# Narrow FoX key tiles in pairs in one score bank, and values multiplied two units behind their scores

## The reference, cut to what matters

```
u = RMSNorm(h); [q,k,v,z]_swa, [q,k,v,z,f]_fox, gate_swa, gate_fox = u @ w_in
y_swa = attention with sinks, ALiBi and a chunked window (8 heads, 2 key heads) * silu(z_swa)
log_f = log_sigmoid(ff + b_forget);  c = cumsum(log_f)
logits[t,s] = q[t].k[s] / 8 + c[t] - c[s],  s <= t;  y_fox = softmax(logits) @ v * silu(z_fox)   (8 heads)
h + RMSNorm((sigmoid(gate_swa) * (y_swa @ w_up_swa) + sigmoid(gate_fox) * (y_fox @ w_up_fox)) @ w_out)
```

## Time and profile before

| | us |
|---|---|
| median of 3 runs | 812.93 |
| lowest, highest | 811.78, 816.03 |
| the profiled execution, its own time | 811.67 |
| its span, first to last instruction | 809.9 |
| mean granted TensorE clock | 0.999 |

### The profile page before, as it was taken

The page is one execution under the profiler, slowest core; times in us unless marked ns, Lnnn a source line. Parts: engine busy times, 40 slices in busy tenths (PEclk is TensorE's granted clock), DMA queues, the critical chain, the costliest instruction groups (busy, mean ns, idle before and its releaser), DMA issues.

```text
span 809.9 us, 11838 instructions
## 1 busy us (share of the span) xinstructions
PE 789.2 (97%) x4058; PEld 624.0 (77%) x4058; DVE 481.1 (59%) x1006; ACT 315.4 (39%) x650; POOL 340.7 (42%) x287
## 2 busy tenths in 40 slices
PE   6999999999999999999999999999998999999996
PEld 4998889888888888888888865655554788878885
DVE  6835258577787777645646366677777634441222
ACT  6534022343334333333334337666767122231111
POOL 1132300765445535444445325758766335512221
PEclk9999999999999999999999999999999999999999
DMA  9344114479955435344344598999800665352222
GB/s 279 107 142 112 51 41 132 135 188 246 215 141 152 111 91 152 99 122 117 99 129 121 140 280 217 232 230 232 192 1 14 224 179 157 104 207 79 104 78 79
DMA packets 127813, 116.02 MB, mean 143 GB/s; under 512 B 29693, under 2 KB 102221, under 8 KB 127754
## 3 DMA queue, kind: packets, MB, share of 16 engines
q1 hardware_dynamic: 126456, 111.53, 51.8%
q10 hardware_dynamic: 1298, 3.74, 1.2%
HBM read 81.99 MB, written 34.96 MB: 144 GB/s over the span
## 4 chain that ended last, share of the span: by engine, by line
PE 88%; issue 4%; POOL 3%; DVE 3%; ACT 2%; DVEq 0%; ACTq 0%; POOLq 0%
PE PS L1986 21%; PE PS L1987 21%; PE PS L1988 21%; PE PS L2270 4%; PE PS L2272 4%; PE PS L2271 4%; PE PS L2192 3%; PE PS L2131 2%; POOL acc L1307 2%; PE PS L2172 1%; PE PS L2207 1%; PE PS L2173 1%; PE PS L2223 1%; PE PS L2018 1%; ACT p_fox L1480 1%
## 5 line engine op out<-in xcount | busy, mean ns | idle before, releaser
L1234 POOL TENSOR_TENSOR ops<-s_sum,ops 128x512 fp32r<-128x512 f32 x64 | 91.3, 1436 | 96.7 <-ACT ops L1336 96.7
L1234 POOL TENSOR_TENSOR ops<-raw,ops 128x512 fp32r<-128x512 f32 x48 | 67.9, 1416 | 118.8 <-ACT ops L1336 118.4
L1986 PE MATMUL PS<-t_hi,ops 128*128 128x512 f32 x256 | 100.1, 391 | 0.0
L1988 PE MATMUL PS<-t_hi,ops 128*128 128x512 f32 x256 | 99.9, 390 | 0.0
L1987 PE MATMUL PS<-t_lo,ops 128*128 128x512 f32 x256 | 99.9, 390 | 0.0
L1307 POOL TENSOR_TENSOR acc<-acc,p_fox 128x400 f32<-128x400 f32 (+5 forms) x76 | 61.4, 830 | 6.9 <-ACT p_fox L1480 5.8
L1480 ACT ACTIVATE p_fox<-PS,neg_c_col 128x512 f32<-128x512 f32 (+5 forms) x112 | 54.3, 536 | 13.0 <-PE PS L2178 8.5
L1804 DVE TENSOR_TENSOR z_tmp<-u,PS 128x512 f32<-128x512 f32 x48 | 32.9, 686 | 42.7 <-PE PS L1988 23.5
L1336 ACT ACTIVATE ops<-s_sum 128x512 fp32r<-128x512 f32 x64 | 39.4, 623 | 47.9 <-DVE s_sum L1588 42.8
L1988 PEld LDWEIGHTS PS<-t_hi,ops 128*128 128x128 f32 x256 | 48.1, 188 | 10.3
L1457 ACT ACTIVATE stage_b<-z_tmp,half_bg 128x512 f32<-128x512 f32 x32 | 23.2, 725 | 82.9 <-DVE z_tmp L1804 82.9
(11 more groups left out here) (237 smaller groups left out, 2040.9 us busy)
## 6 DMA issues: line engine op xcount, KB each, us to landing
raw<-in_w_in_dram SPq DMA_DIRECT2D x34, 512.0 KB, 5.3
g_dram<-stage_b SPq DMA_DIRECT2D x32, 256.0 KB, 2.0
tanh_g<-g_dram SPq DMA_DIRECT2D x16, 512.0 KB, 4.0
x_all<-in_x_dram SPq DMA_DIRECT2D x8, 512.0 KB, 7.3
raw<-in_w_in_dram SPq DMA_DIRECT2D x16, 256.0 KB, 4.7
q_dram<-stage_b SPq DMA_DIRECT2D x16, 256.0 KB, 2.8
q_swa_dram<-stage_b SPq DMA_DIRECT2D x16, 256.0 KB, 2.9
z_dram<-stage_b SPq DMA_DIRECT2D x16, 256.0 KB, 2.0
```

What stands on the lines that cost most here:

```text
L1234: nc.gpsimd.tensor_tensor(ops[:, i % OPS, 1], op_source(p, name), ops[:, i % OPS, 0].bitcast(F32), ALU.subtract).then_inc(op_ready, 1)
L1986: pe.matmul(dst, hi_w, hi, start=first, stop=False)
L1988: return pe.matmul(dst, lo_w, hi, start=False, stop=last)
```

## The change

A unit may now hold two narrow tiles side by side in one score bank: 400 with 16 columns, and 272 with 144. Half 0 has three units, half 1 seven, so a pair has 10 and the stage 40. Scores, exponentials, values and adds stay one instruction (or set) for each tile; semaphores are counted by unit. The mask matmul now comes right behind its head's scores. The last tile of half 0 has 16 keys, not 128. The adds (a step of their own now, `acc`) stay one unit behind the scores; the values on PE are two units behind (LAG). Items get one unit each, from unit 2 to unit 33. The tables of turns are set for 10 units; den stays two units behind the last tile.

```diff
+LAG = 2
 PROB_RING = 3
 FIRST_SLOT = 2
-REC_UNITS = ((4, 5, 6, 7, 8), (2, 3, 4, 5, 5))
-SECOND_LOADS = ((2, "load_queries", 0), (3, "load_keys", 0), (4, "load_values", 0), (8, "load_z", 0),
-                (9, "load_keys", 1), (10, "load_queries", 1), (11, "load_values", 1), (12, "load_z", 1))
+UNITS = (((0,), (1, 4), (2, 3)), ((0,), (1,), (2,), (3,), (4,), (5, 8), (6, 7)))
+REC_UNITS = ((4, 5, 6, 7, 7), (2, 3, 3, 4, 4))
+SECOND_LOADS = ((2, "load_queries", 0), (2, "load_keys", 0), (3, "load_values", 0), (6, "load_z", 0),
+                (7, "load_keys", 1), (8, "load_queries", 1), (9, "load_values", 1), (9, "load_z", 1))
 EARLY_UPS = 2
-SPLIT_TURNS = ((1, 0, 0, 1), (2, 1, 0, 1), (3, 2, 0, 1), (4, 3, 0, 1), (6, PAIRS + 2, 0, 2), (9, 0, 1, 2), (9, 1, 1, 2),
-               (10, 2, 1, 2), (10, 3, 1, 2), (11, PAIRS, 0, 2), (12, PAIRS + 1, 0, 2))
-NEXT_LOADS = ((1, "load_queries", None), (3, "load_keys", None), (5, "load_values", None), (6, "load_z", None))
+SPLIT_TURNS = ((1, 0, 0, 1), (2, 1, 0, 1), (2, 2, 0, 1), (3, 3, 0, 1), (4, PAIRS + 2, 0, 2), (7, 0, 1, 2), (7, 1, 1, 2),
+               (8, 2, 1, 2), (8, 3, 1, 2), (9, PAIRS, 0, 2), (9, PAIRS + 1, 0, 2))
+NEXT_LOADS = ((1, "load_queries", None), (2, "load_keys", None), (3, "load_values", None), (4, "load_z", None))
+UP_TURNS = (2, 4, 6, 8)
...
-    keys = min(P, LENGTH - P * i)
+    keys = min(P, r0 + w + N_META - P * i)
...
+def unit_tiles(q, tiles):
+
+    out, at = [], 0
+    for i in tiles:
+        r0, w, keys, masked, shift = key_tile(q, i)
+        out.append((i, at, r0, w, keys, masked, shift))
+        at += w
+    assert at <= BANK
+    return out
...
-    units = [(j, q, i) for j in range(PAIRS) for q in range(2) for i in range(4 * q + 5)]
+    units = [(j, q, tiles) for j in range(PAIRS) for q in range(2) for tiles in UNITS[q]]
     per = len(units) // PAIRS
-    spread = len(units) - 8 - FIRST_SLOT
+    spread = ITEMS
...
-        if u:
-            pj, pq, pi = units[u - 1]
-            steps.append(dict(kind="values", j=pj, q=pq, i=pi, u=u - 1, first=pi == 0, last=pi == 4 * pq + 4))
+        for kind, back in (("acc", 1), ("values", LAG)):
+            if u >= back:
+                steps.append(of_unit(kind, u - back))
...
-        if split_ups and not slot and (j >= 2):
+        if j == 2 and x in UP_TURNS:
...
+    for kind, back in (("values", 2), ("acc", 1), ("values", 1)):
+        steps.append(of_unit(kind, len(units) - back))
...
+                        for k, (i, at_, r0, w, keys, masked, shift) in enumerate(st["tiles"]):
+                            c0 = r0 - BANK * q
+                            dst = acc[0:keys, f % 2, h, c0:c0 + w]
+                            tile = p_fox[0:keys, n % PT_RING, at_:at_ + w]
+                            if q == 0 and i == 0:
+                                nc.gpsimd.tensor_copy(dst, tile).then_inc(acc_done["pool"], 1)
+                                continue
+                            other = p_fox[:, (n - 2) % PT_RING, :] if (q, i) == (1, 1) else dst
+                            if (n, k) in acc_before:
+                                pool.wait_ge(*acc_before[n, k])
+                            nc.gpsimd.tensor_tensor(dst, other, tile, ALU.add).then_inc(acc_done["pool"], 1)
...
-                        nc.scalar.activation(p_fox[0:keys, n % PT_RING, 0:w],
-                                             PS[0:keys, S_BANKS[n % S_RING], 0:w], ACT.Exp,
-                                             bias=neg_c_col[0:keys, i, 2 * j + h:2 * j + h + 1],
-                                             scale=1.0).then_inc(fox_exp, 1)
+                        for i, at_, r0, w, keys, masked, shift in st["tiles"]:
+                            ins = nc.scalar.activation(p_fox[0:keys, n % PT_RING, at_:at_ + w],
+                                                       PS[0:keys, S_BANKS[n % S_RING], at_:at_ + w], ACT.Exp,
+                                                       bias=neg_c_col[0:keys, i, 2 * j + h:2 * j + h + 1], scale=1.0)
+                        ins.then_inc(fox_exp, 1)
...
-                        pe.matmul(dst, KA[n][:, h, kk], QA[n][:, h, tok], start=True, stop=False)
-                        ins = pe.matmul(dst, KB[n][:, h, kk], QB[n][:, h, tok], start=False, stop=not masked)
-                        if not masked:
-                            ins.then_inc(tile_done, 1)
-                    if masked:
-                        for h in range(2):
-                            pe.matmul(PS[0:keys, S_BANKS[(2 * u + h) % S_RING], 0:masked], causal[:, 0:keys],
-                                      ident_b[:, shift:shift + masked], start=False, stop=True).then_inc(tile_done, 1)
+                        for i, at_, r0, w, keys, masked, shift in st["tiles"]:
+                            tok, kk = slice(r0, r0 + w), slice(P * i, P * i + keys)
+                            bank = PS[0:keys, S_BANKS[x % S_RING], :]
+                            dst = bank[:, at_:at_ + w]
+                            pe.matmul(dst, KA[n][:, h, kk], QA[n][:, h, tok], start=True, stop=False)
+                            ins = pe.matmul(dst, KB[n][:, h, kk], QB[n][:, h, tok], start=False, stop=not masked)
+                            if masked:
+                                ins = pe.matmul(bank[:, at_:at_ + masked], causal[:, 0:keys],
+                                                ident_b[:, shift:shift + masked], start=False, stop=True)
+                        ins.then_inc(tile_done, 1)
...
-                        ins = pe.matmul(PS[h * HEAD:(h + 1) * HEAD, Y_BANKS[f % 2], c0:c0 + w],
-                                        VF[j % 2][0:keys, i, h * HEAD:(h + 1) * HEAD],
-                                        p_fox[0:keys, x % PT_RING, 0:w], start=st["first"], stop=st["last"])
+                    for k, (i, at_, r0, w, keys, masked, shift) in enumerate(st["tiles"]):
+                        c0 = r0 - BANK * q
+                        for h in range(2):
+                            ins = pe.matmul(PS[h * HEAD:(h + 1) * HEAD, Y_BANKS[f % 2], c0:c0 + w],
+                                            VF[j % 2][0:keys, i, h * HEAD:(h + 1) * HEAD],
+                                            p_fox[0:keys, (2 * u + h) % PT_RING, at_:at_ + w], start=i == 0,
+                                            stop=st["last"] and k == len(st["tiles"]) - 1)
```

More of the change, by code:

```diff
@@ L257, in key_tile, with of_unit @@
     return r0, w, keys, masked, shift
+def unit_tiles(q, tiles):
[6 more added lines that the diff above has]
+    return out
 def attention_steps():
     steps = []
+    def of_unit(kind, u):
+        j, q, tiles = units[u]
+        return dict(kind=kind, j=j, q=q, i=tiles[0], u=u, tiles=unit_tiles(q, tiles), last=tiles == UNITS[q][-1])
     def score(i):
@@ L279, in attention_steps @@
     closing = []
-    for u, (j, q, i) in enumerate(units):
-        first, last = i == 0, i == 4 * q + 4
+    for u, (j, q, tiles) in enumerate(units):
+        last = tiles == UNITS[q][-1]
         x = u % per
-        steps.append(dict(kind="tile", j=j, q=q, i=i, u=u, first=first, last=last))
+        steps.append(dict(kind="tile", j=j, q=q, i=tiles[0], u=u, tiles=unit_tiles(q, tiles)))
         if j + 1 < PAIRS:
@@ L287, in attention_steps @@
                     steps.append(dict(kind=what, j=j + 1, u=u, part=part))
[L288 to L289 removed]
+        if (j, x) in ((1, 5), (1, 7)):
+            steps.append(dict(kind="load_up", d=(x - 5) // 2, u=u))
         untransposed, normed = normed, unnormed
@@ L332, in attention_steps @@
                     steps.append(dict(kind="split_y", s=part, c0=c0, c1=c1))
-            if x == 13:
+            if x == per - 1:
                 steps.append(dict(kind="split_y", s=2 * PAIRS - 1, c0=0, c1=1))
-    j, q, i = units[-1]
-    steps.append(dict(kind="values", j=j, q=q, i=i, u=len(units) - 1, first=False, last=True))
+    for kind, back in (("values", 2), ("acc", 1), ("values", 1)):
+        steps.append(of_unit(kind, len(units) - back))
     for _, extra in closing:
@@ L834, in q_column @@
             return q_scale[:, j:j + 1] if kind == "qs" else q_scale[:, PAIRS:PAIRS + 1]
-        unit_of = {x: u for u, x in enumerate(units)}
+        last_unit = {(j, q): u for u, (j, q, tiles) in enumerate(units)}
         Q0, Q1 = slice(0, HEAD), slice(HEAD, P)
@@ L1284, in _ @@
                                             ALU.mult).then_inc(swa_normed, 1)
-                elif kind == "values":
+                elif kind == "acc":
                     j, q, i, u = st["j"], st["q"], st["i"], st["u"]
                     f = 2 * j + q
-                    r0, w, keys, masked, shift = key_tile(q, i)
-                    c0 = r0 - BANK * q
                     if i == 0 and f >= 2:
@@ L1886, in _ @@
                                                    scalar=0.5, in1=yy, op0=ALU.mult, op1=ALU.mult).then_inc(swa_y, 1)
-                elif kind == "values" and acc_by.get(2 * st["u"] + 1) == "dve":
```

(9 more changed lines are left out.)

39 lines of the change are left out of this document (14 added, 25 removed).

## The result

The changed kernel takes 821.94 us by the median of 6 runs (818.68 to 823.51), beside 813.16 for the kernel before on the same chip: ratio 1.0104, 95% interval 1.0076 to 1.0131. It is slower by some 8.5 us, where no change was forecast, and it lies above the range. Its profiled execution took 820.62 us with a span of 819.0; that of before 811.67 with 809.9.

A forecast was written before the change was run, and what follows sets the result against it. TensorE, 97% busy, was taken as the bound, with the load stream holding item 16: 546.8 + 77.3 + 4.3 = 628.4 against 626.6, less 0.2, so +1.6 and 814.5 us by the median; range 808 to 820.

The forecast's parts named there:

- The sign that was named with the gate: Before item 16's SWA score: a TensorE hole of 2 us or more, ending on a QBs landing near 546.8.
- the gate: At item 16: token tile 4's QBs still lands at 546.74, so TensorE waits and time gained earlier is given back.
- one sign of being wrong: At the attention stage's end: ending after 633 us with waits for acc would show the forecast wrong.
- From item 16 on: Item 16 to first projection matmul: 77.3 us of work, against 79.8 in the old kernel, with 4.3 of new holes added.
- The clock is at its upper level, 1.00, throughout: TensorE's clock in the attention stage, read from the old kernel's trace; no clock loss was put in the sum.
- New holes, "4.3 us": Behind item 16: denominators wait 1.0 us in unit 31, 2.2 in unit 34, last SWA values 1.1; bounds 2 to 9.
- less 10 merges x 0.2: Merged score and values steps behind item 16: 0.2 us saved for a pair, 2.0 in all.
- B: Slower: GpSimd's accumulator adds at the half boundaries become the bound, holes 9 us instead of 4.3, 819; chance 0.23.
- A: Faster: loads land earlier, so item 16 isn't held, or holes behind it are small; 809.5 by the median; chance 0.17.
- C: No effect another way: values' waits turn up at the score banks; within 1 us of forecast, counted in its 0.60.
- Even with 3 us of new holes it stands before item 16 at about 544 and waits some 3 us: TensorE ahead of item 16: reached at 541.3 us with the old holes, so slack remains before the 546.74 landing.

The follow-up runs named there:

- load_order: Changed kernel with values and z of the next whole pair loaded one unit later, behind token tile 4's SWA queries: 819.88 us, 1.0076.
- up_turns: Changed kernel with the four early projection-weight splits moved to units 24 to 27 of pair 2: 817.36 us, 1.0060.
- tile_order: Changed kernel with scores issued tile by tile, both heads ahead of the two mask matmuls, as in the kernel before: 818.57 us, 1.0070.
- pool_order: Changed kernel with GpSimd doing its accumulator adds ahead of the SWA normalisation in every unit: 817.14 us, 1.0050.
- single_load: Single-unit kernel with lag two, early tile 1 queries and GpSimd's adds first, plus next pair's values and z loaded one unit later: 814.28 us, 1.0011.
- late_load: Changed kernel with moved splits, adds first, masks behind both heads, early tile 1 queries, items over 33 units, later values and z loads: 806.54 us, 0.9924.

## Why the prediction was wrong

**Right.** Item 16 started on the landing, at 547.46 for a landing at 547.42 (546.7 forecast for both), and no sooner than in the kernel before. Item 4 was reached near 494.6 and waited for QBs (3.1 us; 2.9 follows from the forecast's 493.5 and 496.4). The waits for ScalarE went. GpSimd's pair units take 3.95 us (0.87 + 3.08) for the 3.9 forecast; the denominators' waits at units 31 and 34 came out at 1.0 and 2.3, for 1.0 and 2.2. That the stream runs at what the earlier trace rows show and not at the figure of the Trainium skill, "DMA: Bandwidth & Descriptors", section Bandwidth (about 358 GB/s), held too: 229 to 245 GB/s from 490 to 546 us in four of the kernels.

**Half right.** The sign that was named with the gate, a hole of 2 us or more ahead of item 16, is missing: the wait there was 0.3 us. Item 8 did not wait for its landing either (514.26 for a landing at 512.55). So the gate held the changed kernel for 0.3 us only, and three of the repaired ones for 3.8 to 4.8; load_order, where QBs landed no earlier, tells nothing on it. And one sign of being wrong came true, a stage that ends after 633 us with waits for acc.

**Wrong.** "From item 16 on" was forecast at 77.3 + 4.3 = 81.6 us and took 88.0. Term by term:

- *"The clock is at its upper level, 1.00, throughout"* was read from the kernel before and carried over. Holes of 2 us were forecast and nobody asked what the clock does behind them. The two falls behind item 16 cost 1.6 to 1.7 us each by the steps inside them: +3.3. This is the largest single term, and the one whose kind was missed.
- *New holes, "4.3 us"*: 5.7 by the distance between starts. Units 31 and 34 cost 1.2 and 2.5, near the forecast. Unit 24 cost 2.0, where the sum has nothing: the new table of turns puts a split on GpSimd into unit 22; the prediction counted GpSimd's adds and normalisation there and left out the split. up_turns shows it. The last SWA values, 1.1 in the sum, hardly waited. Together +1.4.
- *"less 10 merges x 0.2"*, that is 0.14 for merged values and 0.05 for merged scores. Scores of 400 and 16 took 1.53 us where this gives 0.93 + 0.45 - 0.05 = 1.33, those of 272 and 144 took 1.36 as forecast (1.50 the last time). Values of 400 and 16 took 1.04 for 0.90, those of 272 and 144 0.75 for 0.87. Over the steps behind item 16 the scores of the pairs come to +1.2 (a wait of 0.15 us in it) and their values to +0.1. The diff also moves each mask between the heads and the narrow tile behind its wide one; the prediction passed over the order, and tile_order shows that the order alone is 0.28, 0.09 and 0.08 us a step. Why the order costs that wasn't tried.
- *The other steps*: tiles of 512 came to +0.8 (masked ones 1.17 for 1.09), SWA scores to -0.4 (0.52 behind tiles without a mask, where 0.61 was taken). With the pairs that makes +1.7 for all steps.

The sum is 3.3 + 1.4 + 1.7 = 6.4, and 6.4 was measured. It is the account of one execution; that the clock falls in the others too is shown by their mean clocks only.

**The rivals.** B named the mechanism, the denominators waiting for the adds of the pair unit behind a normalisation that waits for VectorE, and pool_order confirms it. Its condition, more than about 2 us at three of the four boundaries, was not met (2.3, 1.8, 1.0 and none), yet the time came out beyond its own: it was priced without the clock at 819, and had 0.23. A's condition, loads that land earlier than now, didn't come true (QBs of tile 4 landed at 547.42). C's waits at the score banks don't show in the changed kernel's list. "Even with 3 us of new holes it stands before item 16 at about 544 and waits some 3 us" failed by the same terms as the sum: a hole of 3.1 us, a fall of 1.7, smaller waits and dearer steps brought it there at 547.2.

## What to carry to other kernels

Price a new hole in TensorE's stream not by its length alone: look in the windows at the granted clock behind the longest holes, and where the kernel before has none as long, ask what comes behind the first. Read the order of matmuls inside a merged step as a change of its own, and every table of turns for what it puts on the engine that is about to be waited for. A transfer that holds the order hides the gains ahead of it: here three repairs that gained singly gave half together, and nearly all once the transfer itself landed earlier. And when one wait goes, look for the next one behind it before judging a second edit: here the wait of the last SWA values, with its fall, was worth as much as the one at the gate.

## What the runs showed of the hardware

The falls of the granted clock inside the stage last 3.41 us or twice that (6.83), at 0.50. The twenty traces have 30 of them there. 26 began during a wait of TensorE of 1.8 us or more or less than 2 us behind its end; the other four, all in kernels of single units (as at 530 in single_load), had no wait above 0.9 us in the 3 us before them. Taken the other way, the waits of 3.0 us and more, eleven of them, all had a fall with them; of the 24 waits from 1.8 to 2.9 us 15 had one and 9 had none, such as the 2.9 us for VF at 506 in late_load. The wait of 1.84 us at unit 24 had a fall in one of four kernels. So a long hole makes a fall likely here, single executions differ, and no bound is shown.

Second, the same SWA queries, with the load order up to them unchanged, landed 5.6 to 7.5 us after their issue in different kernels and executions: in three from 490.31 to 496.10, in load_order from 490.58 to 498.04. Item 4's wait was 1.8 us in the one and 3.6 in the other, which may be a part of the 3 us by which single runs of these kernels differ. Loaded ahead of z they took 4.6 to 5.4 us.
